# Where the recurrence's running products are computed: moved from GpSimd to VectorE, with the low halves of two weight units

## The reference

```
b = jnp.cumsum(gc, axis=2)
diff = jnp.where(causal, b[:, :, :, None, :] - b[:, :, None, :, :], -jnp.inf)
att = jnp.einsum('bhtk,bhsk,bhtsk->bhts', qc, kc, jnp.exp(diff))
out = jnp.einsum('bhtk,bhkv->bhtv', qc * jnp.exp(b), S) + jnp.einsum('bhts,bhsv->bhtv', att, vc)
S = jnp.exp(b_last[:, :, 0, :])[..., None] * S + jnp.einsum('bhsk,bhsv->bhkv', kc * jnp.exp(b_last - b), vc)
```

## Time and profile before

| | |
|---|---|
| three runs, median | 1621.9 us (1617.07 to 1624.07) |
| the profiled execution | 1623.42 us, span 1621.6 us |
| TensorE matmuls busy | 1556.8 us, 96% |
| VectorE busy | 1106.1 us, 68% |
| ScalarE busy | 641.5 us, 40% |
| GpSimd busy | 686.5 us, 42% |
| levels of group 0, group 1 | about 687 to 725 us, 760 to 795 us of the span |

### The profile page before, as it was taken

The page is one execution under the profiler, slowest core; times in us unless marked ns, Lnnn a source line. Parts: engine busy times, 40 slices in busy tenths (PEclk is TensorE's granted clock), DMA queues, the critical chain, the costliest instruction groups (busy, mean ns, idle before and its releaser), DMA issues. The chain is left out here.

```text
span 1621.6 us, 30580 instructions
## 1 busy us (share of the span) xinstructions
PE 1556.8 (96%) x12309; PEld 1432.0 (88%) x12309; DVE 1106.1 (68%) x1621; ACT 641.5 (40%) x1173; POOL 686.5 (42%) x559
## 2 busy tenths in 40 slices
PE   9899999999989999999999889998998999999998
PEld 7899999999957999988887656558998999999998
DVE  7998877874317689886847443336568988778752
ACT  5354444443452324422243433331244454444431
POOL 4244444446521335682624323344443444444441
PEclk9999999999999999997999999999999999999999
DMA  7233332333611322322333488996232233323322
GB/s 192 60 83 94 95 105 82 89 94 115 217 32 42 104 72 80 98 73 72 99 111 140 163 318 342 415 364 243 79 94 63 72 105 97 99 73 92 108 76 72
DMA packets 195756, 203.68 MB, mean 126 GB/s; under 512 B 6928, under 2 KB 182096, under 8 KB 187168
## 3 DMA queue, kind: packets, MB, share of 16 engines
q1 hardware_dynamic: 175712, 107.91, 23.3%
q0 software_dynamic: 12256, 77.93, 12.6%
q10 hardware_dynamic: 7648, 15.89, 2.6%
HBM read 187.21 MB, written 14.30 MB: 124 GB/s over the span
## 5 line engine op out<-in xcount | busy, mean ns | idle before, releaser
L2282 PE MATMUL ps<-b_lo,w_hi 128*128 128x288 f32 x1064 | 313.7, 295 | 6.5 <-ACT snap L977 3.1
L2284 PE MATMUL ps<-b_hi,w_hi 128*128 128x288 f32 x1064 | 315.5, 296 | 0.0
L711 POOL TENSOR_TENSOR w_lo<-raw,w_hi 128x512 fp32r<-128x512 f32 x114 | 174.0, 1533 | 240.7 <-DVE sum_f L1490 121.4
L696 POOL TENSOR_TENSOR w_lo<-raw,w_hi 128x512 fp32r<-128x512 f32 (+1 forms) x122 | 168.6, 1414 | 191.7 <-ACT w_hi L910 191.6
L910 ACT ACTIVATE w_hi<-raw 128x512 fp32r<-128x512 f32 (+4 forms) x265 | 201.8, 765 | 106.3 <-PE ps L2157 82.3
L2157 PE MATMUL ps<-hid_hi,w_hi 128*128 128x288 f32 x704 | 209.6, 298 | 0.0
L2155 PE MATMUL ps<-hid_lo,w_hi 128*128 128x288 f32 x704 | 208.4, 296 | 0.0
L2156 PE MATMUL ps<-hid_hi,w_lo 128*128 128x288 f32 x704 | 208.1, 296 | 0.0
L2282 PEld LDWEIGHTS ps<-b_lo,w_hi 128*128 128x128 f32 x1064 | 199.8, 188 | 8.4 <-ACT w_hi L910 3.7
L2284 PEld LDWEIGHTS ps<-b_hi,w_hi 128*128 128x128 f32 x1064 | 200.1, 188 | 0.0
L703 POOL TENSOR_TENSOR w_lo<-raw,w_hi 128x512 fp32r<-128x512 f32 x112 | 132.6, 1195 | 157.4 <-ACT w_hi L910 156.2
(11 more groups left out here) (363 smaller groups left out, 3737.5 us busy)
## 6 DMA issues: line engine op xcount, KB each, us to landing
raw<-in_ffn_w_gate SPq DMA_DIRECT2D x44, 512.0 KB, 3.9
raw<-in_ffn_w_up SPq DMA_DIRECT2D x44, 512.0 KB, 5.3
raw<-in_w_in SPq DMA_DIRECT2D x22, 1024.0 KB, 5.2
raw<-in_ffn_w_down SPq DMA_DIRECT2D x48, 384.0 KB, 3.4
gates<-scratch_g ACTq DMA_DIRECT2D x4, 1152.0 KB, 10.1
raw<-in_ffn_w_down SPq DMA_DIRECT2D x16, 256.0 KB, 3.3
raw<-in_w_out SPq DMA_DIRECT2D x4, 1024.0 KB, 5.2
scratch_x<-xT ACTq DMA_DIRECT2D x1, 2304.0 KB
```

Source lines behind the costliest of these rows:

```text
L696: ins = pool.tensor_tensor(raw_unit(u, w_lo)[:, part], raw_unit(u, raw)[:, part], hi_unit(u)[:, part].bitcast(F32), ALU.subtract)
L711: pool.tensor_tensor(raw_part(u, m, w_lo), raw_part(u, m, raw), in_four(hi_block(u, b)).bitcast(F32), ALU.subtract).then_inc(S("w_lo_done" ...
L2282: pe.matmul(dst, hi[:, i * P:(i + 1) * P], x_lo, start=begin, stop=False, skip_group_check=True)
L2284: ins = pe.matmul(dst, hi[:, i * P:(i + 1) * P], x_hi, start=False, stop=end, skip_group_check=True)
```

## The change

The four multiplies of each level go to VectorE. `decays(g, L)` is called after both heads' `q_lev`, `k_lev` and `att` copies of the level, first `left` for the two heads, then `decay` for the two. After those of levels 3 to 6 VectorE computes one quarter of `w_lo` of gate unit 2g+1 (`gate_low`). GpSimd waits for that unit's `w_lo` to be done before it goes on to the next unit, keeps the state transfers, and in group 1 issues the loads of heads 2 and 3 directly behind the stores of heads 0 and 1.

```diff
-            def decays(g):
-                for L in range(1, len(LEVELS)):
-                    for a in range(2):
-                        b = LEVELS[L]
-                        end, mid, first, right = level_views(2 * g + a, L)
-                        pool.wait_ge(S(f"level_in{a}"), 8 * g + L)
-                        if L > 1:
-                            pool.wait_ge(S(f"decayed{a}"), 2 * (7 * g + L - 1))
-                        pool.tensor_tensor(first, first, end, ALU.mult).then_inc(S(f"decayed{a}"), 1)
-                        pool.wait_ge(S(f"decayed{a}"), 2 * (7 * g + L - 1) + 1)
-                        pool.tensor_tensor(right, right, mid, ALU.mult).then_inc(S(f"decayed{a}"), 1)
-                    if 3 <= L <= 6:
-                        low_part(L - 3)
-                    if g and L == 2:
-                        state_load(2)
-                        state_load(3)
-
             state_load(0)
             state_load(1)
             for g in range(2):
-                decays(g)
+                if g:
+                    state_load(2)
+                    state_load(3)
+                pool.wait_ge(S("w_lo_done"), LO_AT[at_unit["gate", 2 * g + 1], 0])
+                done[0] += 1
                 lows(at_unit["gate", 2 * g + 2 if g == 0 else 4])
...
+            def decays(g, L):
+                for part in range(2):
+                    for a in range(2):
+                        end, mid, first, right = level_views(2 * g + a, L)
+                        if part == 0:
+                            dve.wait_ge(S(f"level_in{a}"), 8 * g + L)
+                            dve.tensor_tensor(first, first, end, ALU.mult).then_inc(S(f"decayed{a}"), 1)
+                        else:
+                            dve.wait_ge(S(f"decayed{a}"), 2 * (7 * g + L - 1) + 1)
+                            dve.tensor_tensor(right, right, mid, ALU.mult).then_inc(S(f"decayed{a}"), 1)
+
+            def gate_low(u, m):
+                if m == 0:
+                    dve.wait_ge(S("w_hi_done"), HI_AT[u, 0])
+                part = slice(BLOCK * m, BLOCK * m + BLOCK)
+                ins = dve.tensor_tensor(raw_unit(u, w_lo)[:, part], raw_unit(u, raw)[:, part],
+                                        hi_unit(u)[:, part].bitcast(F32), ALU.subtract)
+                if m == 3:
+                    ins.then_inc(S("w_lo_done"), 1)
...
                         if L - 1 < ACT_LEVEL:
                             level_out(a, L - 1)
+                    decays(g, L)
+                    if 3 <= L <= 6:
+                        gate_low(at_unit["gate", 2 * g + 1], L - 3)
```

## The result

Five runs of the changed kernel took 1606.22 to 1611.16 us, median 1608.4, against 1619.91 us before. The ratio is 0.9934 with a 95% interval of 0.9918 to 0.9950. Faster, by 10.7 us by the ratio, where 6.8 were forecast. The profiled execution had a span of 1608.0 us, against 1621.6. In two later comparisons of the same kernel the ratio was 0.9959 (0.9942 to 0.9975) and 0.9935 (0.9918 to 0.9951), gains of 6.6 and 10.5 us. Two of the 6.6 us between the forecast 1615 and 1608.4 are the base's: five runs of the kernel before have their median at 1619.9, three had it at 1621.9.

A forecast was written before the change was run, and what follows sets the result against it. GpSimd, slowing VectorE to half, sets the period in levels 4 to 6 of a TensorE program. Gains 4.1 + 3.1 = 7.2 us, trimmed to 7.0, then 6.8 for the clock: 1615 against the median 1621.9, range 1608 to 1621.5.

The forecast's parts named there:

- The price of a moved instruction: On VectorE, GpSimd idle, start to start: 0.34 us for 256 columns, 0.37 for 288, 0.60 for a 512-column quarter.
- The sum over the levels: VectorE from level 2's first q_lev to the last products: 23.9 us, before 27.3 in group 0 and 26.3 in group 1.
- Rival 1: Moved VectorE instructions don't overlap and cost full durations: levels 26.0 us, 3 us gained, time 1619; chance 0.18, shared with another rival.
- TensorE as a follower: TensorE's need, 3.4 us in levels 4 to 7, stays under every VectorE level but the seventh; 0.2 us taken off.
- The last pair: VectorE's q_lev/k_lev pair of 576 columns after the levels, faster without GpSimd: 0.7 us gained for the pair.
- The gain of level 1: Nothing: the moved multiplies fill VectorE's waits before level 2, 1.54 us in group 0 and 2.89 us in group 1.
- No gain or loss from the transfers: Sample state transfers move some 10 us earlier, feed products after the levels, and cost nothing.
- the gain should persist to the end: Everything behind the levels is relative to TensorE's progress, so the gain lasts, though the clock there may change it.
- the clock: TensorE's slow clock in group 0 would fall beside VectorE's longest level: at most 0.5 us against the gain.
- rival 2: Shorter TensorE idle keeps 2.4 GHz in group 0 and part of 725 to 760 us: 3.5 us more, time 1611; chance 0.19.
- Rival 3: TensorE's clock falls inside the levels, about 5.4 us a level: 14 us lost less 7, time 1629; chance 0.05.
- would win nearly nothing: Adding up the page's full VectorE instruction durations, without overlap between starts, the change would gain almost nothing.

The follow-up runs named there:

- no_gap: The change with the products ordered left, decay for head 0, then left, decay for head 1, each decay directly after its producer; 1614.7 us, ratio to before 0.9974.
- loads_late: The change with the state loads of the last two heads issued after level 2, as in the kernel before; 1614.4 us, ratio to before 0.9960.
- quarters_only: The kernel before with only the quarters of w_lo moved to VectorE, the multiplies staying on GpSimd; 1619.2 us, ratio to before 0.9998.
- early_in_group1: The change, but group 1's four w_lo quarters go back to GpSimd, all at once beside level 1; 1614.9 us, ratio to before 0.9976.
- rows_first: The change with ScalarE copying k_rows before it rounds the next gate unit; 1613.4 us, ratio to before 0.9961.
- stall_level1: The change with six more dependent memsets of left on VectorE in level 1, head 1, group 0; 1620.5 us, ratio to before 1.0003.
- quarters_early: The change with each group's four w_lo quarters done by GpSimd at once, ahead of or beside level 1; 1617.4 us, ratio to before 0.9994.

## Why the prediction was right, and by how much

The mechanism was right: VectorE's levels, priced without GpSimd beside them, and a gain that reached the end. The size of the first result was in part luck.

- The price of a moved instruction, 0.34, 0.37 and 0.60 us from start to start with GpSimd idle: measured 0.34, 0.37 and 0.60.
- The sum over the levels, 23.9 us: measured 23.85 and 24.01 in every run of the change. Rival 1, no overlap for the moved instructions, would have been 26.0. Part of its mechanism exists, 0.12 us a pair in no_gap, and the order left, left, decay, decay avoids it.
- TensorE as a follower: it was the bound only in level 2 of group 1, which took 4.43 us where VectorE's list has 4.22. Its waits for `att`, written down as 0.3 to 0.6 us a level, were 0.2 us once in each group. In levels 2 to 5 it shows no idle time, so less slack than counted.
- The last pair, counted at 0.7 us a group: from the last products to the last transpose 3.57 and 3.58 us before, 2.80 and 2.80 after.
- The gain of level 1, nothing: in group 0 VectorE was at level 2 in 4.13 us from the first `att` copy (691.36 to 695.49) against 4.28 before. In group 1 it was 5.38 us against 6.17, 0.8 us that the sum did not have. The repeats had 5.73 and 5.32 us, loads_late 6.13: it goes with TensorE's pace, for which VectorE waits there. With it the two groups gained 8.2 us in the profiled pair, where the sum had 7.0.
- No gain or loss from the transfers: none shown, but loads_late leaves up to 4 us open.
- Behind the levels, "the gain should persist to the end": for the change it did. For smaller gains it was not seen: the loops of quarters_only are 2.4 us shorter in sum and the whole is not, and early_in_group1 is 1.8 us shorter in its loop and slower as a whole.
- The term that was off was the clock. It was set at at most 0.5 us against the gain and, in rival 2, at 3.5 us for it with a chance of 0.19. Rival 2's time (1611) is nearer to the first result than the forecast, but not for its reason. It wanted the lost time back in the levels of group 0 and in their tail. In the levels of group 0 about 1.7 us did come back. The tail of group 0 did not change: a clock of 0.82 before, 0.84, 0.85 and 0.84 in the three profiles of the change. What made the first pair of profiles 13.6 us apart was the clock in the tail of group 1 and behind 820 us, which no case of the prediction named, and which differs between executions of one kernel.
- How much of the gain is the moved work can be estimated from the executions with a mean clock on record. The kernel before (81) has a mean of 1619.4 us at 0.9822, the change (19) 1610.6 us at 0.9850. A run gets shorter by 0.9 us within the change, and by 0.8 us within the kernel before, for each 0.001 of mean clock. At the same clock of 0.982 the two lines give 1619.5 and 1613.3: 6.2 us for the moved work, forecast 6.8. This is an estimate from two fitted lines.
- That the change itself raises the clock is not shown. Its three sets of runs have 0.9870, 0.9826 and 0.9865. But loads_late and rows_first, with the same loops, have 0.9818 and 0.9819, as the kernel before. The stretch at half clock inside group 0's levels is gone in the three profiles of the change (1.00, where the kernel before had 0.95), but loads_late has it again (0.95).
- Rival 3 did not come. Its slow levels exist: stall_level1 and quarters_early had them behind idle times of 1.55 and 3.5 us, with the reservation above. The price it set, 5.4 us a level at 1.2 GHz, was too low: 6.84 us in quarters_early. The idle time of 0.7 us that it feared in level 3 did not show: TensorE is busy all of the 4.86 us of that level in both groups.
- The sentence that the durations added up "would win nearly nothing" does not fit the sum of rival 1, which is the same case and has 3 us.

## What to carry to other kernels

When GpSimd and VectorE both have elementwise work with two SBUF inputs, look at the distances between starts of the same instruction beside a busy and beside an idle GpSimd before counting how much either can take: here 64 more instructions on VectorE took 2.2 us more of it. Order dependent instructions of one engine so that one independent instruction stands between. And compare a change of this size over many executions with their granted clock, not by two profiles: a shorter loop in a profile is not yet a shorter kernel.

## What the runs showed of the hardware

VectorE's instructions with two SBUF inputs and GpSimd's stand for each other. Beside GpSimd instructions that wait for semaphores in between, a pair of VectorE's products took 1.46 to 1.70 us in place of 0.75. Beside a string of four without a wait (4.97 us) a single one took 5.14 us, though in another run instructions came through inside such a string. VectorE's own unbroken row held a quarter on GpSimd for 6.42 us. A copy with one SBUF input was slowed as well (0.77 us in place of 0.24). A masked copy that reads PSUM is as long beside a busy GpSimd as without (0.41 to 0.44 us).

TensorE's granted clock was 0.50 behind an idle time of 3.5 us and behind one of 1.55 us, the latter with 0.59 standing ahead of it too. It also fell from 1.00 (731 to 735 us) to 0.56 (735 to 739 us) in the tail of group 0 of the kernel before, right behind sixteen matmuls of 8 columns (L2600), and in the same place of the change. Behind the same sixteen in group 1 of the change's first profile it stayed at 1.00, so they alone do not decide it. Summed over slices of 4 us the change lost 21.4, 32.8 and 23.1 us to the clock in its three profiles, and the kernel before 30.2.
